# A place of its own for expert 60's weights: gate and up ahead of expert 3, down behind expert 11

## The chip, the core and the metric

One NeuronCore of a Trainium2 chip runs the kernel. Its engines are TensorE (PE), VectorE (DVE), ScalarE (ACT), GpSimd (POOL) and SyncE (SP); here SP does nothing but issue transfers. The metric is the device time of one execution in microseconds, as the median of the timed runs. One execution is taken apart by the profiler; its rows are quoted below.

## The reference

A two-layer trunk (layer 0 mixes with GLA, layer 1 with sparse attention), each layer followed by a mixture of 64 experts, for 256 prompt tokens and 8 samples. What matters here is the mixture: every token takes 8 of 64 experts, all weights are float32, and each expert is three matrices of 1 MB.

```python
N_EXPERTS = 64; TOP_K = 8; EXPERT_FF = 256; SHARED_FF = 256; D_MODEL = 1024

def swiglu(x, w_g, w_u, w_d):
    return (jax.nn.silu(x @ w_g) * (x @ w_u)) @ w_d

def moe_ffn(h, w_router, router_bias, w_gate, w_up, w_down, ws_gate, ws_up, ws_down):
    ...
    _, eidx = lax.top_k(jnp.where(emask, sel, -jnp.inf), TOP_K)
    wsel = jnp.take_along_axis(s, eidx, axis=-1)
    wsel = wsel / jnp.sum(wsel, axis=-1, keepdims=True) * ROUTE_SCALE
    y = routed_experts(x, eidx, wsel.astype(x.dtype), w_gate, w_up, w_down) + swiglu(x, ws_gate, ws_up, ws_down)

def reference(...):
    for i in range(DEPTH):                      # DEPTH = 2
        ...                                     # mixer, residual
        xp = xp + gt2p[:, None, :] * moe_ffn(modulate(xp, norm_ffn[i], sh2p, sc2p), *mo)
        xs = xs + gt2s[:, None, :] * moe_ffn(modulate(xs, norm_ffn[i], sh2s, sc2s), *mo)
    y_prompt = rms_norm(xp, norm_final)
    y_sample = rms_norm(xs, norm_final)
```

## The kernel before

Each engine runs its own program, written out in order; semaphores hold them together. In each layer a router picks the experts and makes, for each expert, a list of at most 64 tokens; tokens beyond that go to overflow chunks, which come in pairs after expert 63 (two pairs in layer 0, one in layer 1). An even and an odd expert form a pair: POOL gathers the pair's token rows (`gather`, L1828), TensorE transposes them (`pe_turn_half`, L1431), computes gate and up (L1484), transposes the product (L1496), computes down (L1510), and adds the pair before with one-hot matmuls (`pe_add`, L1439). A call of `pe_body` is one expert. Below, e58 is expert 58, and "expert 60 starts" means its first matmul of L1484.

The weights stream through `ring`, four slots (`WS = 4`) of three thirds of 2048 words per partition: gate, up, down. `load_expert` (L1233) issues three transfers on SP, one per third. `sp_experts_first` loads e0 to e3, each as soon as its slot is released by earlier work; the slot of e3 is the one that held the shared expert's weights, released at the end of the router (L1373). In `sp_experts` the load of expert n waits for expert n-4 to be done (semaphore `y`). All SP transfers stand in one queue, in the order of issue. In layer 1 the weight row of the final norm (`sp_final_weight`, L2617) is issued between the loads of e2 and e3.

`main_and_overflow` (L1522) is what TensorE, VectorE, ScalarE and GpSimd share: the first eight experts are unrolled (`apart = 2` rounds of four), then a loop takes four experts a round, then a loop takes the overflow pairs. In the unrolled part the token lists of later experts are still being made between the experts (`pe_between`, `dve_list`, `dve_sel`); the semaphore `lists` counts seven of them per layer.

TensorE waits for an expert's gate, up and down at one place, ahead of L1484:

```python
            wait_alone(pe, wsem, wval)
            gu = ring[:, s, 0:2, :].rearrange("p g (k n) -> p g k n", k=KT)
```

Gate and up lie next to each other in a slot, so one matmul of L1484 covers 128 columns of both (256 moving columns); the two halves of 64 output partitions alternate. In the trace each such float32 matmul stands as two records.

Of the kernel before, what the change touches and what calls it, by code (L numbers as in the profile page):

```python
# [24 lines left out]
P = 128  # L25
D = 1024
KT = D // P
# [5 lines left out]
NE, TOPK, NG, TOPG, FF = 64, 8, 8, 4, 256  # L33
CAP = 64
# [8 lines left out]
WS = 4  # L43
THIRD = 2048
# [110 lines left out]
def build(nc, ins, outs):  # L155
    ctx = ExitStack()
    with ctx:
# [5 lines left out]
        def S(name):  # L163
            if name not in sems:
                sems[name] = ctx.enter_context(nc.semaphore(name))
            return sems[name]
# [100 lines left out]
        def plan(n, signals=True, at=None):  # L267

            got = []
            for i in range(n):  # L270
                s = W.slot() if at is None else at[i % len(at)]
                W.loads[s] += 1
                prior[(s, W.loads[s])] = W.uses[s]
                W.uses[s] += signals
                got.append((s, W.loads[s]))
            return got
# [49 lines left out]
        it_sh = [plan(1)[0], None]  # L326
        after = [(it_sh[0][0] + i) % WS for i in range(1, WS)]
        it_ada[1] = plan(4, at=after)
        it_ex = [plan(NE, False, at=after[1:] + after[:1] + [it_sh[0][0]]), None]
        def hold(s):  # L330

            W.uses[s] += 1
# [6 lines left out]
        hold_v = hold(sd)  # L339
        it_dout = plan(2, at=[sb_, sa])  # L340
        it_sh[1] = plan(1, at=[sd])[0]
        it_ex[1] = plan(NE, False, at=[sb_, sc_, sa, sd])

        hk, hv = GH * GDK, GH * GDV
        w_in = ins["gla_w_in"][0]
# [836 lines left out]
        OH8 = [tk(DEC) for _ in range(2)]  # L1182
        iot = tk(TOK)
        Sel = arena[:, tk.at[0]:tk.at[0] + 1344].bitcast(BF16).rearrange("p (t m n) -> p t m n", t=TT, m=7)
        s_, sel, c1, c2, msk, rep = (tk(TT, NE) for _ in range(6))
        gm = tk(24, 8)
        Mf, Wt = tk(TT, NE), tk(TT, NE)
# [4 lines left out]
        Qall, Rall, Rres = tk(TT, NB), tk(TT, NB), tk(TT, NB)  # L1192
        MV = tk(NB, TT, 5, dt=BF16)
        QT, RT = tk(TT, P), tk(TT, P)
        cnt, nch, base, ovt = tk(1), tk(1), tk(1), tk(4)
        OV, OVb, OVc = tk(NOV), tk(NOV), tk(NOV)
        Lp = tk(NB // 2, 5)
# [26 lines left out]
        def M(l, name):  # L1224
            return S(f"{name}_{l}")
# [4 lines left out]
            return [wg.rearrange("(p k) n -> p (k n)", k=KT), wu.rearrange("(p k) n -> p (k n)", k=KT),  # L1230
                    wd.rearrange("(k p) n -> p k n", p=P)]

        def load_expert(s, e, l, sem):  # L1233
            for t, src in enumerate(expert_w(l, e)):
                dst = ring[:, s, t, :]
                if t == 2:
                    dst = dst.rearrange("p (k n) -> p k n", k=2)
                sp.dma_start(dst, src).then_inc(sem, 16)
# [13 lines left out]
        def sp_experts_first(l):  # L1252
            for u in range(WS):
                s, n = it_ex[l][u]
                sp.wait_ge(S(f"slot_used{s}"), prior[it_ex[l][u]])
                load_expert(s, u, l, S(f"slot_loaded{s}"))
                if l and u == 2:
                    sp_final_weight()

        def sp_experts(l):  # L1260
            with sp.Fori(1, NE // WS) as i:
                for u in range(WS):
                    s = it_ex[l][u][0]
                    sp.wait_ge(M(l, "y"), i * WS + (u - WS + 1))
                    load_expert(s, i * WS + u, l, S(f"slot_loaded{s}"))
            sp.wait_ge(S("lists"), PER["lists"] * l + 7)
            n2 = sp.value_load(npr[0:1, 0:1], min_val=1, max_val=NOV // 2)
            with sp.Fori(0, n2) as i:
                later = (i + 31) >> 5
                for u in range(2):  # L1270
                    e = sp.value_load(eid[0:1, ds(i * 2 + u, 1)], min_val=0, max_val=NE - 1)
                    sp.wait_ge(M(l, "y"), later * 2 + i * 2 + (NE - WS + u + 1))
                    load_expert(it_ex[l][u][0], e, l, M(l, f"over_loaded{u}"))
            sp.wait_ge(M(l, "y"), n2 * 2 + NE)


        def route_pe(eng, l, name):
# [190 lines left out]
        def pe_body(l, i, n, h2, u, s, wsem, wval, over):  # L1468

            b = u % 2  # L1470
            par = 1 if over else u // 2
            last = None if isinstance(h2, int) and h2 == 0 else h2 - 1

            def add(*chunks):
                if last is not None:
                    pe_add_pair(l, last, 1 if over else 1 - par, chunks, (1 if over else 4) in chunks)
            if b == 0:
                pe.wait_ge(M(l, "xgT"), h2 * 2 + 2)
            wait_alone(pe, wsem, wval)
            gu = ring[:, s, 0:2, :].rearrange("p g (k n) -> p g k n", k=KT)  # L1480
            rows = xgT[0 if over else par]
            for k in range(KT):
                for half in range(2):
                    m = pe.matmul(PS[64 * half:64 * half + 64, 5, 0:256].rearrange("p (g n) -> p g n", g=2), rows[:, k, CAP * b:CAP * b + CAP],  # L1484
                                  gu[:, :, k, half * P:(half + 1) * P], start=(k == 0), stop=(k == KT - 1), skip_group_check=True)
            m.then_inc(M(l, "gu"), 1)
            if isinstance(n, int):
                pe_between(l, n)
            if not over and b == 0:
                if isinstance(n, int):  # L1490
                    pe_bank6(l, n)
                pe_turn_half(l, h2 + 1, 1 - par, i + par, 0)
            elif not over:
                add(1)
            pe.wait_ge(M(l, "hm"), n + 1)
            pe.transpose(PS[:, 5, 256:384], hm[b], K["ident"]).then_inc(M(l, "th"), 1)  # L1496
            if over and b == 1:
                pe_turn_half(l, h2 + 1, 1, i + NE // 4, 0)
            elif over:
                add(4, 0)  # L1500
            elif b == 0:
                add(0)
            else:
                add(4)
            pe.wait_ge(M(l, "hT"), n + 1)
            if not isinstance(n, int) or n >= 1:
                pe.wait_ge(M(l, "ysb"), n)
            for kk in range(2):
                for j in range(2):
                    m = pe.matmul(PS[64 * j:64 * j + 64, 7, :], hTt[b][:, kk * CAP:(kk + 1) * CAP],  # L1510
                                  ring[:, s, 2, kk * D + 512 * j:kk * D + 512 * j + 512], start=(kk == 0), stop=(kk == 1), skip_group_check=True)
            m.then_inc(M(l, "y"), 1)
            if over and b == 0:
                add(1)
            elif over:
                pe_turn_half(l, h2 + 1, 1, i + NE // 4, 1)
            elif not over and b == 0:
                pe_turn_half(l, h2 + 1, 1 - par, i + par, 1)
# [3 lines left out]
        def main_and_overflow(eng, l, body, between=None):  # L1522

            for i in range(apart):
                for u in range(WS):
                    body(i, i * WS + u, i * 2 + u // 2, u, False)
            if between is not None:
                between()
            with eng.Fori(apart, NE // WS) as i:
                for u in range(WS):  # L1530
                    body(i, i * WS + u, i * 2 + u // 2, u, False)
            eng.wait_ge(S("lists"), PER["lists"] * l + 7)
            n2 = eng.value_load(npr[0:1, 0:1], min_val=1, max_val=NOV // 2)
            with eng.Fori(0, n2) as i:
                for u in range(2):
                    body(i, i * 2 + (NE + u), i + NE // 2, u, True)
            return n2

        def pe_experts(l):
            def body(i, n, h2, u, over):  # L1540
                s, first = it_ex[l][u]
                if over:
                    pe_body(l, i, n, h2, u, s, M(l, f"over_loaded{u}"), i * 48 + 48, over)
                else:
                    pe_body(l, i, n, h2, u, s, S(f"slot_loaded{s}"), i * 48 + 48 * first, over)
            pe_turn_half(l, 0, 0, 0, 0)
            pe_turn_half(l, 0, 0, 0, 1)
            n2 = main_and_overflow(pe, l, body, lambda: pe_bank6(l, WS * apart))
            pe.wait_ge(M(l, "xgT"), n2 * 2 + (NE + 2))
            if l:  # L1550
                pe_gates()
            wait_alone(pe, M(l, "ysb"), n2 * 2 + NE)
            pe.wait_ge(S("oh_last"), l + 1)
            pe_add_samples(OHw[:, SEQ:TOK], ysb[1]).then_inc(S("acc"), 1)
            pe_add(OHw, [ysb[1]], (0, 1)).then_inc(S("acc"), 1)
            if l:
                pe_final_rows(0)
            pe_add(OHw, [ysb[1]], (2, 3)).then_inc(S("acc"), 1)
# [1044 lines left out]
            act.wait_ge(S("kv_out"), 96)  # L2603


        wrow = shT.rearrange("p k t -> p (k t)")[:, 0:D]
        grow = ysb[0]
        xnew = [arena[:, D * i:D * i + D] for i in range(2)]
        row8 = arena[0:DEC, 2112:2112 + D]
# [5 lines left out]
        gate8 = modT2[:, 1, 40:48, 1:9]  # L2615

        def sp_final_weight():  # L2617
            sp.wait_ge(S("mix_out"), 16)
            sp.dma_start(wrow, ins["norm_final"].rearrange("(o n) -> o n", o=1).broadcast_to([P, D])).then_inc(S("dsa_in"), 16)

        def pe_gates():
# [223 lines left out]
```

## Time and profile before

| | us |
|---|---|
| timed runs, median of 3 | 1615.74 (1615.34 to 1617.96) |
| the profiled execution | 1616.23 |
| its span, first to last instruction | 1614.40 |
| PE busy | 1537.5 (95%) |
| DVE, ACT, POOL busy | 570.2, 438.7, 145.8 |
| bytes moved by DMA | 553.13 MB, mean 343 GB/s |

The page cuts the span into 40 slices of 40.4 us. The expert loop of layer 0 runs from about 271 to 806 us, that of layer 1 from about 1078 to 1593 us; the first is preceded by the GLA layer, the second by the attention layer. A busy PE is not PE at its peak, since matmuls are pipelined; the distance from one start to the next of the same kind of work says more than the busy share. DMA rows give the mean busy share of the 16 DMA engines (it can come out slightly over 1) and what they moved.

### The profile page before, as it was taken

To read this page: it belongs to the slowest core of one execution; us is meant where nothing else is said; L and a number is where in the kernel's file an instruction comes from. 1 tells how busy PE (TensorE), PEld (TensorE's weight loads), DVE (VectorE), ACT (ScalarE), POOL (GpSimd) and SP (SyncE) were. 2 spreads that over 40 slices of the span, in tenths; PEclk is the share of its full clock that TensorE was granted. 3 is DMA by queue.
4 is the path that set the end of the run, shared out by engine and by line. 5 is a ranking of instruction groups with operands and counts; after the bars stand their busy time and mean duration, and the time that the engine had idled before them with its cause. 6 is when DMAs were issued, how large, how long until landed. Compare 5 with 4: busy or idle time off the path is not lost.

```text
span 1614.4 us, 28531 instructions
## 1 busy us (share of the span) xinstructions
PE 1537.5 (95%) x10814; PEld 937.8 (58%) x10814; DVE 570.2 (35%) x1709; ACT 438.7 (27%) x975; POOL 145.8 (9%) x208
## 2 busy tenths in 40 slices
PE   5999999999999999999898989999999999999997
PEld 2768665555555555555477767765555555555554
DVE  4124554622122221212236972466222221212223
ACT  1211121222232222232232143312223222222223
POOL 0001301000000000000020051010000000000000
PEclk9999999999999999999999989999999999999999
DMA  9885678999999999999594656379999999999991
GB/s 368 339 343 190 248 286 335 386 402 416 416 417 416 416 416 416 417 415 414 211 328 105 183 169 202 138 277 390 413 417 416 417 416 416 416 417 416 415 410 75
DMA packets 132290, 553.13 MB, mean 343 GB/s; under 512 B 19503, under 2 KB 36861, under 8 KB 93830
## 3 DMA queue, kind: packets, MB, share of 16 engines
q1 hardware_dynamic: 113746, 514.28, 80.5%
q0 software_dynamic: 15472, 35.02, 6.0%
q10 hardware_dynamic: 3012, 3.00, 0.6%
q8 instruction: 41, 0.67, 0.2%
q14 instruction: 19, 0.16, 0.0%
HBM read 563.19 MB, written 8.96 MB: 354 GB/s over the span
## 4 chain that ended last, share of the span: by engine, by line
PE 70%; DMA 19%; DVE 6%; ACT 2%; issue 1%; SPq 1%; ACTq 1%; DVEq 0%
PE PS L1484 21%; DMA ring<-in_moe_w_down 19%; PE PS L1510 11%; PE PS L1439 6%; PE PS L783 5%; PE PS L943 4%; PE PS L1431 2%; PE PS L2046 2%; PE PS L2042 2%; PE PS L470 1%; PE PS L1446 1%; PE PS L1496 1%; PE PS L2098 1%; DVE arena L1714 1%; ACT arena L1796 1%
## 5 line engine op out<-in xcount | busy, mean ns | idle before, releaser
L1484 PE MATMUL PS<-ring,arena 128*64 128x256 f32 x4288 | 490.5, 381 | 13.1 <-DMA ring<-in_moe_w_down 8.2
L1484 PEld LDWEIGHTS PS<-ring,arena 128*64 128x64 f32 x4288 | 313.6, 137 | 188.5 <-issue 58.6
L1510 PE MATMUL PS<-ring,arena 128*64 128x512 f32 x1072 | 260.3, 606 | 1.4 <-ACT arena L1798 1.4
L1714 DVE TENSOR_TENSOR arena<-arena,PS 128x128 f32<-128x128 f32 x134 | 38.6, 288 | 500.1 <-ACT arena L1796 500.1
L1806 ACT COPY arena<-PS 64x512 f32<-64x512 f32 x134 | 77.5, 578 | 292.7 <-PE PS L1510 292.7
L1439 PE MATMUL PS<-y_parts,oh_pair 128*128 128x512 f32 x520 | 153.7, 417 | 0.0
L1702 DVE TENSOR_SCALAR y_parts<-arena 128x512 fp32r<-128x512 f32 x130 | 62.9, 483 | 247.3 <-ACT arena L1807 247.3
L1510 PEld LDWEIGHTS PS<-ring,arena 128*64 128x64 f32 x1072 | 65.2, 136 | 130.5 <-issue 100.6
L1796 ACT ACTIVATE arena<-PS 128x128 f32<-128x128 f32 x134 | 37.2, 278 | 338.8 <-PE PS L1484 338.8
L1431 PEld LDWEIGHTS PS<-cst,arena 128*128 128x128 f32 x552 | 71.8, 194 | 80.2 <-issue 78.3
L1826 POOL COPY arena<-arena 128x1 int32 (+1 forms) x71 | 15.0, 212 | 1093.4 <-PE PS L1431 909.0
L1439 PEld LDWEIGHTS PS<-y_parts,oh_pair 128*128 128x128 f32 x520 | 87.5, 188 | 38.8 <-issue 25.3
L1431 PE MATMUL PS<-cst,arena 128*128 128x128 f32 x552 | 97.7, 300 | 2.0 <-ACT arena L1813 1.4
L1704 DVE SCALAR_TENSOR_TENSOR y_parts<-arena,y_parts 128x512 fp32r<-128x512 f32 x130 | 97.7, 752 | 4.6
L783 PE MATMUL PS<-hT,ring 128*128 128x264 f32 x384 | 89.4, 390 | 0.4 <-DVE modT L511 0.4
L1813 ACT COPY arena<-PS 128x512 f32<-128x512 f32 x135 | 79.6, 590 | 26.1 <-PE PS L1431 24.5
L783 PEld LDWEIGHTS PS<-hT,ring 128*128 128x128 f32 x384 | 71.7, 190 | 19.2 <-issue 6.2
L1807 ACT COPY arena<-PS 64x512 f32<-64x512 f32 x134 | 78.0, 582 | 1.6
L1828 POOL DMA_INDIRECT arena<-h_rows,arena x71 | 72.5, 1021 | 61.7 <-POOL arena L1826 58.4
L1798 ACT COPY arena<-PS 128x128 f32<-128x128 f32 x134 | 35.7, 266 | 120.7 <-PE PS L1496 120.7
L943 PE MATMUL PS<-shT,ring 128*128 128x264 f32 x256 | 58.6, 390 | 1.6 <-PE PS L943 0.6
L943 PEld LDWEIGHTS PS<-shT,ring 128*128 128x128 f32 x256 | 48.8, 192 | 11.2 <-issue 1.4
(542 smaller groups left out, 1378.7 us busy)
## 6 DMA issues: line engine op xcount, KB each, us to landing
ring<-in_moe_w_gate SPq DMA_DIRECT2D x134, 1024.0 KB, 11.6
ring<-in_moe_w_up SPq DMA_DIRECT2D x134, 1024.0 KB, 15.9
ring<-in_moe_w_down SPq DMA_DIRECT2D x134, 1024.0 KB, 20.7
ring<-in_w_ada SPq DMA_DIRECT2D x36, 1024.0 KB, 12.4
ring<-in_gla_w_in SPq DMA_DIRECT2D x8, 1152.0 KB, 13.9
ring<-in_w_ada SPq DMA_DIRECT2D x8, 1152.0 KB, 11.9
ring<-in_dsa_w_in SPq DMA_DIRECT2D x6, 1024.0 KB, 20.8
arena<-in_state_gla POOLq DMA_DIRECT2D x8, 512.0 KB, 7.8
```

What stands on the lines that cost most here:

```text
L783: m = pe.matmul(PS[:, b, 0:TOK], w8_[:, k, (m_ % 6) * P:(m_ % 6 + 1) * P], hT[:, k, 0:TOK], start=(k == 0), stop=(k == KT - 1))
L943: m = pe.matmul(PS[:, 4 + k % 4, 0:TOK], w3[:, kk, (k % 2) * P:(k % 2 + 1) * P], src[:, kk, :], start=(kk == 0), stop=(kk == KT - 1))
L1431: ins_ = pe.transpose(PS[:, 6, k * P:(k + 1) * P], xv[:, 4 * half + k, :], K["ident"])
L1439: ins_ = pe.matmul(PS[:, c, :], oh[:, T * P:(T + 1) * P], y[:, 512 * j:512 * j + 512], start=False, stop=True, skip_group_check=True)
L1484: m = pe.matmul(PS[64 * half:64 * half + 64, 5, 0:256].rearrange("p (g n) -> p g n", g=2), rows[:, k, CAP * b:CAP * b + CAP], gu[:, :, k, ...
L1510: m = pe.matmul(PS[64 * j:64 * j + 64, 7, :], hTt[b][:, kk * CAP:(kk + 1) * CAP], ring[:, s, 2, kk * D + 512 * j:kk * D + 512 * j + 512], ...
L1702: dve.tensor_scalar(yR[:, 0, q], ysb[par][:, q], wv[:, par:par + 1], None, ALU.mult).then_inc(M(l, "part"), 1)
L1704: dve.scalar_tensor_tensor(out=yR[:, 1, q], in0=ysb[par][:, q], scalar=wv[:, par:par + 1], in1=yR[:, 0, q], op0=ALU.mult, op1=ALU.subtract ...
L1806: act.copy(ysb[par][q, 0:512], PS[0:CAP, 7, :])
L1807: act.copy(ysb[par][q, 512:D], PS[CAP:P, 7, :]).then_inc(M(l, "ysb"), 1)
L1813: act.copy(xgT[into][:, 4 * half:4 * half + 4, :].rearrange("p k c -> p (k c)"), bank(6)).then_inc(M(l, "xgT"), 1)
L1828: pool.indirect_dma_start(out=xg[into], out_offset=None, in_=hrow_d[l], in_offset=IndirectOffsetOnAxis(ap=gi[:, into:into + 1], axis=0), b ...
```

## The change

Expert 60 (`SPARE = NE - WS`) no longer goes through the ring. Its gate lies in the first 2048 words of `arena`, its up in the first 2048 of `shT`, its down in 2048 words of `arena` that held the router's temporaries (`spare`). Its transfers count on a semaphore of their own (`extra_loaded0`), gate and up are issued ahead of e3's slot wait (`sp_spare_in`), down behind the load of e11 (`sp_spare_down`). For that, SP's rounds for e4 to e11 are unrolled. e61 to e63 take the slots and waits that e60 to e62 had (`order`), the overflow pair takes slots 3 and 0 instead of 0 and 1 (`over_slot`). Since gate and up of e60 are not adjacent, each of its matmuls is split into one for gate and one for up, of 128 moving columns each. On the four compute engines e60 to e63 are unrolled. The final norm's row, in layer 1, moves from behind e2's load to behind e60's down, and from `shT` to another part of `arena`.

```diff
-        it_ex = [plan(NE, False, at=after[1:] + after[:1] + [it_sh[0][0]]), None]
+        SPARE = NE - WS
+        order = lambda e: e - 1 if e > SPARE else e
+        it_ex = [plan(NE - 1, False, at=after[1:] + after[:1] + [it_sh[0][0]]), None]
...
+        spare = [arena[:, 0:THIRD], shT.rearrange("p k t -> p (k t)")[:, 0:THIRD], arena[:, routed_at:routed_at + THIRD]]
...
-        def load_expert(s, e, l, sem):
-            for t, src in enumerate(expert_w(l, e)):
-                dst = ring[:, s, t, :]
+        def load_expert(s, e, l, sem, thirds=range(3)):
+            for t in thirds:
+                dst, src = spare[t] if s is None else ring[:, s, t, :], expert_w(l, e)[t]
...
                 s, n = it_ex[l][u]
+                if u == WS - 1:
+                    sp_spare_in(l)
                 sp.wait_ge(S(f"slot_used{s}"), prior[it_ex[l][u]])
                 load_expert(s, u, l, S(f"slot_loaded{s}"))
-                if l and u == 2:
-                    sp_final_weight()
+
+        def sp_spare_in(l):
+
+            route_pe(sp, l, "e_T")
+            sp.wait_ge(S("mix_out"), KT * (l + 1))
+            load_expert(None, SPARE, l, M(l, "extra_loaded0"), (0, 1))
+
+        def sp_spare_down(l):
+
+            sp.wait_ge(S("lists"), PER["lists"] * l + 7)
+            load_expert(None, SPARE, l, M(l, "extra_loaded0"), (2,))
+            if l:
+                sp_final_weight()
 
         def sp_experts(l):
-            with sp.Fori(1, NE // WS) as i:
+            def load(i, u):
+                sp.wait_ge(M(l, "y"), i * WS + (u - WS + 1))
+                s = it_ex[l][u][0]
+                load_expert(s, i * WS + u, l, S(f"slot_loaded{s}"))
+            for i in range(1, 3):
                 for u in range(WS):
-                    s = it_ex[l][u][0]
-                    sp.wait_ge(M(l, "y"), i * WS + (u - WS + 1))
-                    load_expert(s, i * WS + u, l, S(f"slot_loaded{s}"))
+                    load(i, u)
+            sp_spare_down(l)
+            with sp.Fori(3, NE // WS - 1) as i:
+                for u in range(WS):
+                    load(i, u)
+            for e in range(SPARE + 1, NE):
+                s = it_ex[l][order(e)][0]
+                sp.wait_ge(M(l, "y"), order(e) - WS + 1)
+                load_expert(s, e, l, S(f"slot_loaded{s}"))
...
-                    sp.wait_ge(M(l, "y"), later * 2 + i * 2 + (NE - WS + u + 1))
-                    load_expert(it_ex[l][u][0], e, l, M(l, f"over_loaded{u}"))
+                    sp.wait_ge(M(l, "y"), later * (2 if u else 3) + i * 2 + (NE - WS + 2 * u))
+                    load_expert(over_slot(l, u), e, l, M(l, f"extra_loaded{u}"))
             sp.wait_ge(M(l, "y"), n2 * 2 + NE)
+
+        def over_slot(l, u):
+            return it_ex[l][(NE - 1 + u) % WS][0]
...
             for k in range(KT):
+                if s is None:
+                    for g in range(2):
+                        for half in range(2):
+                            m = pe.matmul(PS[64 * half:64 * half + 64, 5, P * g:P * g + P], rows[:, k, CAP * b:CAP * b + CAP],
+                                          gu[g][:, k, half * P:(half + 1) * P], start=(k == 0 and g == 0), stop=(k == KT - 1), skip_group_check=True)
+                    continue
...
-            with eng.Fori(apart, NE // WS) as i:
+            with eng.Fori(apart, NE // WS - 1) as i:
                 for u in range(WS):
                     body(i, i * WS + u, i * 2 + u // 2, u, False)
+            for u in range(WS):
+                body(NE // WS - 1, SPARE + u, SPARE // 2 + u // 2, u, False)
...
-        wrow = shT.rearrange("p k t -> p (k t)")[:, 0:D]
+        wrow = arena[:, routed_at + THIRD:routed_at + THIRD + D]
...
         def sp_final_weight():
-            sp.wait_ge(S("mix_out"), 16)
```

## Rows read from the trace of the kernel before

**Rows 1.** The page, parts 1 and 2: busy times; GB/s in 40 slices.
```profile
PE 1537.5 (95%) x10814; PEld 937.8 (58%) x10814; DVE 570.2 (35%) x1709; ACT 438.7 (27%) x975; POOL 145.8 (9%) x208
...
GB/s 368 339 343 190 248 286 335 386 402 416 416 417 416 416 416 416 417 415 414 211 328 105 183 169 202 138 277 390 413 417 416 417 416 416 416 417 416 415 410 75
```

**Rows 2.** Timeline of PE (start us, us long, line, form), layer 0, e14 to e16.
```profile
382.09 3.62 PE L1484 MATMUL PS<-ring,arena 128*64 128x256 f32 x32
...
390.20 3.67 PE L1484 MATMUL PS<-ring,arena 128*64 128x256 f32 x32
...
397.35 2.98 PE L1484 MATMUL PS<-ring,arena 128*64 128x256 f32 x26
```

**Rows 3.** Timeline of PE, layer 0, e58 to e62; brackets: idle before, what ended it.
```profile
725.54 3.67 PE L1484 MATMUL PS<-ring,arena 128*64 128x256 f32 x32 [0.19 <-issue]
...
733.73 3.67 PE L1484 MATMUL PS<-ring,arena 128*64 128x256 f32 x32
...
741.37 3.67 PE L1484 MATMUL PS<-ring,arena 128*64 128x256 f32 x32 [0.32 <-DMA ring<-in_moe_w_down]
...
749.55 3.67 PE L1484 MATMUL PS<-ring,arena 128*64 128x256 f32 x32
...
756.70 3.62 PE L1484 MATMUL PS<-ring,arena 128*64 128x256 f32 x32
```

**Rows 4.** Windows, layer 0: stretch, its length, busy by engine, PE clock, DMA share, GB/s.
```profile
276.00:280.00 4.00, 3.98 (x26) 2.04 (x28) 3.53 (x9) 2.20 (x4) 0.84 (x1) 1.00 0.62 208
...
304.00:308.00 4.00, 4.00 (x36) 2.25 (x32) 2.86 (x4) 1.16 (x2) 0.00 (x0) 1.00 0.58 192
308.00:336.00 28.00, 27.94 (x247) 15.76 (x245) 14.73 (x46) 7.81 (x18) 1.98 (x4) 1.00 1.00 403
336.00:366.00 30.00, 29.88 (x212) 16.28 (x210) 7.25 (x18) 8.97 (x20) 3.15 (x5) 1.00 1.01 401
366.00:742.00 376.00, 369.55 (x2556) 203.44 (x2554) 86.89 (x216) 108.50 (x242) 28.68 (x48) 1.00 1.02 416
```

**Rows 5.** DMA issues of the whole run: size of each, median us to landing.
```profile
ring<-in_moe_w_gate SPq DMA_DIRECT2D x134, 1024.0 KB, 11.6
...
shT<-in_norm_final SPq DMA_DIRECT2D x1, 512.0 KB, 18.7
```

**Rows 6.** Timeline of SP's issues, layer 1: the norm's row, then e3's first.
```profile
1047.19 0.52 SPq L2619 DMA_DIRECT2D shT<-in_norm_final  x1
1074.81 0.33 SPq L1238 DMA_DIRECT2D ring<-in_moe_w_gate  x1
```

**Rows 7.** Windows, layer 1, columns as in rows 4.
```profile
1068.00:1075.00 7.00, 6.67 (x32) 2.84 (x30) 5.48 (x12) 0.00 (x0) 0.00 (x0) 1.00 0.01 2
1142.00:1532.00 390.00, 383.81 (x2654) 211.48 (x2652) 90.36 (x225) 112.89 (x252) 29.95 (x51) 1.00 1.02 416
```

**Rows 8.** Timeline of PE, layer 1, e58 to e61.
```profile
1531.59 3.67 PE L1484 MATMUL PS<-ring,arena 128*64 128x256 f32 x32 [0.46 <-DMA ring<-in_moe_w_down]
...
1539.74 3.67 PE L1484 MATMUL PS<-ring,arena 128*64 128x256 f32 x32
...
1547.16 3.67 PE L1484 MATMUL PS<-ring,arena 128*64 128x256 f32 x32
...
1555.34 3.67 PE L1484 MATMUL PS<-ring,arena 128*64 128x256 f32 x32
```

**Rows 9.** Timeline of PE, attention layer: 64 weight columns, 128 moving, alternating halves.
```profile
874.43 3.76 PE L2123 MATMUL PS<-arena 128*64 128x128 f32 x64 [1.12 <-ACT arena L2540]
```

**Rows 10.** e61's down: SP's issue; then size and us to landing (DMA issues, 725 to 727.5).
```profile
726.43 0.38 SPq L1238 DMA_DIRECT2D ring<-in_moe_w_down  x1
...
ring<-in_moe_w_down SPq DMA_DIRECT2D x1, 1024.0 KB, 22.4
```

**Rows 11.** Waits from 540 to 760 us: us in total, times, longest.
```profile
PE PS L1484 <- issue: 3.1, 6, 1.3
```

**Rows 12.** Timeline of PE: the router's transposes of layer 1.
```profile
1043.87 0.37 PE L1308 MATMUL PS<-cst,arena 64*128 64x64 f32 x3
```

More of the change, by code:

```diff
@@ L341, in build @@
         it_sh[1] = plan(1, at=[sd])[0]
-        it_ex[1] = plan(NE, False, at=[sb_, sc_, sa, sd])
+        it_ex[1] = plan(NE - 1, False, at=[sb_, sc_, sa, sd])
         hk, hv = GH * GDK, GH * GDV
@@ L1184, in build @@
         Sel = arena[:, tk.at[0]:tk.at[0] + 1344].bitcast(BF16).rearrange("p (t m n) -> p t m n", t=TT, m=7)
+        routed_at = tk.at[0]
+        spare = [arena[:, 0:THIRD], shT.rearrange("p k t -> p (k t)")[:, 0:THIRD], arena[:, routed_at:routed_at + THIRD]]
         s_, sel, c1, c2, msk, rep = (tk(TT, NE) for _ in range(6))
@@ L1194, in build @@
         QT, RT = tk(TT, P), tk(TT, P)
+        assert tk.at[0] >= routed_at + THIRD + D
         cnt, nch, base, ovt = tk(1), tk(1), tk(1), tk(4)
@@ L1479, in pe_body @@
             wait_alone(pe, wsem, wval)
-            gu = ring[:, s, 0:2, :].rearrange("p g (k n) -> p g k n", k=KT)
+            gu = ([spare[g].rearrange("p (k n) -> p k n", k=KT) for g in range(2)] if s is None
+                  else ring[:, s, 0:2, :].rearrange("p g (k n) -> p g k n", k=KT))
+            wd = spare[2] if s is None else ring[:, s, 2, :]
             rows = xgT[0 if over else par]
             for k in range(KT):
+                if s is None:
[4 more added lines that the diff above has]
+                    continue
                 for half in range(2):
@@ L1510, in pe_body @@
                     m = pe.matmul(PS[64 * j:64 * j + 64, 7, :], hTt[b][:, kk * CAP:(kk + 1) * CAP],
-                                  ring[:, s, 2, kk * D + 512 * j:kk * D + 512 * j + 512], start=(kk == 0), stop=(kk == 1), skip_group_check=True)
+                                  wd[:, kk * D + 512 * j:kk * D + 512 * j + 512], start=(kk == 0), stop=(kk == 1), skip_group_check=True)
             m.then_inc(M(l, "y"), 1)
@@ L1542, in body @@
                 if over:
-                    pe_body(l, i, n, h2, u, s, M(l, f"over_loaded{u}"), i * 48 + 48, over)
+                    pe_body(l, i, n, h2, u, over_slot(l, u), M(l, f"extra_loaded{u}"), i * 48 + (48 if u else 96), over)
+                elif isinstance(n, int) and n == SPARE:
+                    pe_body(l, i, n, h2, u, None, M(l, "extra_loaded0"), 48, over)
+                elif isinstance(n, int) and n > SPARE:
+                    s, nth = it_ex[l][order(n)]
+                    pe_body(l, i, n, h2, u, s, S(f"slot_loaded{s}"), 48 * nth, over)
                 else:
```

## The prediction

> **What bounds the kernel now.** I read the page's busy times and slices first, then the timeline of TensorE at three places of the expert loops, then windows of the DMA engines, then the issues on SP. The page [rows 1] gives TensorE 95% of the span, and slices 9 to 18 and 28 to 38 move 415 GB/s or so: through both expert loops two resources are full at once, and the question is which of them ends last at each expert.
>
> In the middle of a loop it is TensorE. From one expert's first gate/up matmul to the next it takes 8.11 us after an even expert and 7.15 us after an odd one [rows 2], 15.26 us for a pair, and nothing is waited for. The weights come more slowly: an expert is three transfers of 1024 KB [rows 5], and with the gathered token rows between them the queue, at a flat 416 GB/s from 366 to 742 us [rows 4], does not keep up. So the lead that the four slots had at the start is used up, and later each even expert waits a little for its down weights: e58 to e60 of layer 0 take 8.19 and 7.64 us, 15.83 for the pair [rows 3].
>
> What is decisive is where that ends. After e60 the strides are 8.18 and 7.15 us [rows 3], those of TensorE alone. Expert 60 is the last one that the stream delays; from there to the loop's end the time is TensorE's own. Layer 1 is the same: 7.42 us from e59 to e60, 8.18 to e61, with a wait ahead of e58 [rows 8].
>
> **The change, part by part.** Times are set against the profiled execution, 1616.23 us with a span of 1614.40; the median of the timed runs is 0.49 us lower.
>
> *Bytes moved.* At 416 GB/s a transfer of 1024 KB costs 1,048,576 / 416,000 = 2.52 us, one of 512 KB 1.26 us. Expert 60's gate and up (5.04 us of stream) go ahead of e3's load, its down (2.52 us) behind e11's, and in layer 1 the final norm's row (512 KB, 1.26 us [rows 5]) goes from ahead of e3 to behind that down. All experts from e12 to e59 are behind these in one queue. Let d be by how much later their weights land. What was e60's turn in the queue is now e61's, so e61 and all behind it come some 5 us earlier against their need; but there TensorE sets the pace, and nothing is won by it.
>
> *d in layer 1.* SP issues the norm's row at 1047.19 and then nothing until 1074.81 [rows 6]; from 1068 to 1075 us the DMA engines move 2 GB/s [rows 7]. Gate and up need 5.04 us of that and the row leaves it, so they are free. Down and the row land in a stretch (1142 to 1532 us) that runs at 416 GB/s without a hole [rows 7]: d = 2.52 + 1.26 = 3.78 us. Below, I bound it by 2.52, if the row, one line read for all partitions, should cost nothing.
>
> *d in layer 0.* Here e3 follows e2 closely, so gate and up push e3 back; e3 has time, and what counts is which holes they fill later. Measured as bytes missing to 416 GB/s, the windows 276 to 280 and 304 to 308 us hold 4 x (1 - 208/416) = 2.00 and 4 x (1 - 192/416) = 2.15 us; 308 to 336 holds 0.87 and 336 to 366 1.08 us; after that, nothing [rows 4]. If a deeper queue wins all of it back, gate and up are absorbed by 336 (5.02 of 5.04 us) and of the down 2.52 - 1.08 = 1.44 us stay: d = 1.46. If only the idle share of the two holes counts, 4 x (1 - 0.62) + 4 x (1 - 0.58) = 3.20 us, d = 7.56 - 3.20 = 4.36. I take the two holes in full and half of the two shallow windows, because in these the engines are already busy and only the rate is low: d = 7.56 - 4.15 - 0.98 = 2.4 us.
>
> *What d does at the end.* The last expert that waits is now e58, since e60's weights are there. It starts d later; e59 follows as before, e60 at TensorE's 7.15 us. Against before, the waits ahead of e60 and e61 are gone: 7.64 - 7.15 and 8.18 - 8.11, 0.56 us in layer 0 [rows 2, 3]; 7.42 - 7.15 and 8.18 - 8.11, 0.34 us in layer 1 [rows 2, 8].
>
> *Two-piece matmuls.* Expert 60's gate and up are no longer side by side, so 16 matmuls of 256 columns become 32 of 128, 64 records in place of 32. The trace has just this form, 64 columns of weights on alternating halves with 128 moving columns: 64 records in 3.76 us [rows 9], against 3.67 us for the 32 [rows 2]. That is 0.09 us a layer, all on TensorE's path. The Trainium skill (TensorE: Matmul & The Clock Gate, Back-to-back issue gap) speaks against such a split: sustained, it gives about 81 ns a matmul at 128 columns, because weight loading then sets the spacing. By that, an estimate from the page, 64 records would take 5.2 us and the change would cost 1.5 us a layer more than the 3.67; the row with the same form decides here.
>
> *Unrolling and waits.* Four bodies a layer stand unrolled on each engine and one round of the loop goes; I cost it at nothing, since it is the same instructions. Below nothing there is no room: across the loop's turn, from e15 to e16, the stride is the bare 7.15 us [rows 2]. From above I take the longest idle time ahead of a gate/up matmul that the trace leaves to issue, 1.3 us [rows 11], once a layer. SP's new waits are met before it comes to them. Gate and up wait for the router's transposes (L1308), in layer 1 at 1043.87 us, and SP is there at 1047.19 [rows 6, 12]; were they late, e3's load would stand behind. The down's is for the last of the seven lists, which VectorE makes within e7's body, while e11's load, ahead of it on SP, waits until e7 is done; were it late, e12's load would stand behind it. The overflow loads move from slots 0 and 1 to 3 and 0; the second pair's first load still waits for the first pair's first expert.
>
> *Sum.* Layer 0: 2.4 - 0.56 + 0.09 = +1.93 us. Layer 1: 3.78 - 0.34 + 0.09 = +3.53 us. Together +5.5 us: 1621.7 for the profiled execution, **1621.2 us** for the median, 0.34% slower. With both lower ends (1.46 and 2.52) it is +3.3 us, with the upper one (4.36) and 1.3 us a layer for issue +10.0.
>
> **The rivals.**
>
> *The stream sets the end, and the change is faster.* If what follows e60 hangs on the stream and not on TensorE, each layer gains what left the busy part: 5.04 us less what layer 0 cannot absorb, and 5.04 - 1.26 in layer 1, up to 8.8 us: 1606.9 us. For it: e61's down is issued at 726.43 and lands 22.4 us later, 0.7 us before e61 starts [rows 3, 10], so after e60 both are close. Against it: being early by 0.7 us is not being late, and the strides are the bare ones of rows 2. The point from which it decides is a wait ahead of e62 or later; there is none. Chance 0.10.
>
> *The waits are a round trip and not a rate, and nothing changes.* Each wait of the loop could be that of four slots: a slot is released, and its new weights land 22 us later, whatever else is queued. Then one more transfer behind e11 delays nobody (d = 0), and the loss of the waits at e60 gives -0.56 - 0.34 + 0.18 = -0.7 us: 1615.0 us. The Trainium skill (Perfetto Trace Analysis, Optimization Strategy) has this reading: a gap that repeats can mean that there are too few buffers for the next tile. By that rule a fifth home is the right remedy; the trace disagrees here, with 416 GB/s whether experts wait or not. Against it speaks that flat rate [rows 4, 7]: the queue is full, and a full queue passes a delay on. Chance 0.10. Another 0.10 for within 0.2% comes from the lower ends of the forecast.
>
> *Slower by more.* The unrolled tail stalls on its code, or split matmuls cost more than the row says: 1624.5 us and beyond. Chance 0.08. The forecast itself, above 0.2%, has 0.62.
>
> **How the numbers follow.** About 0.2%, 3.2 us, is what a measurement of this kernel can tell from no change. Faster by more: 0.10. Within: 0.10 + 0.10 = 0.20. Slower by more: 0.62 + 0.08 = 0.70. The forecast's own range is 1619.0 to 1624.5. The range for 8 in 10 takes in the round-trip case and leaves out the faster rival and what lies above: 1615.0 to 1624.5.
>
> **What would show it.** Right: e58 still waits for its down weights and starts some 2.4 us (layer 0) and 3.8 us (layer 1) later against the loop's first expert; the first waits come at an earlier expert of each loop; e60 to the loop's end runs at 7.15 and 8.1 us with weights landed long before; expert 60's gate/up take 3.8 us. Wrong: e58 not later, which is the round trip; strides under 7.15 us after e60, which is the faster rival; a gap between the loop and e60, which is code.

## The result and the profile after

| | before | after |
|---|---|---|
| median of 20 runs each, us | 1617.17 (1612.5 to 1622.0) | 1622.55 (1615.4 to 1626.54) |
| ratio, with its 95% interval | | 1.0033 (1.0022 to 1.0044) |
| profiled execution, and its span, us | 1616.23, 1614.40 | 1620.23, 1618.4 |

The change makes the kernel 0.33% slower: 5.4 us by the medians, 3.6 to 7.1 by the interval. The prediction was 1621.2 us, 5.5 us over the median of three runs of before that it started from (1615.74); twenty runs put that median at 1617.17. It was right, and the runs below say how far for its reasons.

The page of after, parts 1 and 2, beside [rows 1]: TensorE is as busy as before, and both loops still move 415 to 417 GB/s once they are under way. Fuller are above all the slices around the loops' starts, counted from 0 as in the prediction: 6 and 7 (366 and 403 GB/s for 335 and 386) and 26 and 27 (318 and 397 for 277 and 390).

```profile
PE 1537.6 (95%) x10878; PEld 939.9 (58%) x10878; DVE 569.4 (35%) x1709; ACT 438.7 (27%) x975; POOL 146.1 (9%) x208
...
GB/s 369 336 344 190 247 288 366 403 407 417 416 417 416 417 416 417 416 415 390 169 326 109 179 169 216 144 318 397 405 417 416 417 416 416 416 416 417 415 377 32
```

SP's issues in after (start us, us, line): gate and up of expert 60, then e3's first load, in layer 0 and in layer 1. They go out 8.8 us before e3's in layer 0 and 27.7 us before it in layer 1.

```profile
259.25 0.39 SPq L1243 DMA_DIRECT2D arena<-in_moe_w_gate  x1
259.68 1.22 SPq L1243 DMA_DIRECT2D shT<-in_moe_w_up  x1
268.06 0.33 SPq L1243 DMA_DIRECT2D ring<-in_moe_w_gate  x1
...
1047.56 0.41 SPq L1243 DMA_DIRECT2D arena<-in_moe_w_gate  x1
1048.01 0.46 SPq L1243 DMA_DIRECT2D shT<-in_moe_w_up  x1
1075.24 0.33 SPq L1243 DMA_DIRECT2D ring<-in_moe_w_gate  x1
```

Windows of after, columns as in [rows 4]. The two early holes of layer 0 are nearly gone (411 and 369 GB/s for 208 and 192), the idle stretch of layer 1 moves 83 GB/s for 2, and the long stretches stand at 416 as before [rows 4, 7].

```profile
276.00:280.00 4.00, 3.65 (x23) 1.77 (x24) 3.88 (x11) 2.32 (x5) 0.84 (x1) 1.00 1.01 411
...
304.00:308.00 4.00, 4.00 (x34) 2.25 (x32) 3.27 (x5) 1.16 (x2) 0.00 (x0) 0.99 0.96 369
308.00:336.00 28.00, 27.94 (x247) 15.76 (x245) 14.73 (x46) 7.81 (x18) 1.74 (x3) 1.00 0.99 393
336.00:366.00 30.00, 29.89 (x212) 16.34 (x210) 7.24 (x18) 8.97 (x20) 3.40 (x5) 1.00 1.02 413
366.00:742.00 376.00, 368.25 (x2544) 203.48 (x2540) 86.83 (x216) 107.62 (x240) 28.68 (x48) 1.00 1.02 416
...
1068.00:1075.00 7.00, 7.00 (x32) 3.00 (x30) 5.86 (x13) 0.00 (x0) 0.00 (x0) 1.00 0.22 83
...
1142.00:1532.00 390.00, 381.62 (x2634) 211.32 (x2631) 90.28 (x225) 111.83 (x249) 30.37 (x51) 1.00 1.02 416
```

TensorE's timeline in after (L1523 is gate/up from the ring, L1519 the two-piece form of e60): e58 to e63 of layer 0, then e58 and e59 of layer 1.

```profile
728.53 3.67 PE L1523 MATMUL PS<-ring,arena 128*64 128x256 f32 x32
...
736.69 3.67 PE L1523 MATMUL PS<-ring,arena 128*64 128x256 f32 x32
...
743.84 0.39 PE L1519 MATMUL PS<-arena 128*64 128x128 f32 x4
744.05 0.39 PE L1519 MATMUL PS<-shT,arena 128*64 128x128 f32 x4
...
747.11 0.39 PE L1519 MATMUL PS<-shT,arena 128*64 128x128 f32 x4
...
751.90 3.67 PE L1523 MATMUL PS<-ring,arena 128*64 128x256 f32 x32
...
759.05 3.62 PE L1523 MATMUL PS<-ring,arena 128*64 128x256 f32 x32
...
767.07 3.67 PE L1523 MATMUL PS<-ring,arena 128*64 128x256 f32 x32
...
1535.33 3.67 PE L1523 MATMUL PS<-ring,arena 128*64 128x256 f32 x32 [0.26 <-DMA ring<-in_moe_w_down]
...
1543.49 3.67 PE L1523 MATMUL PS<-ring,arena 128*64 128x256 f32 x32
```

e58 is late and still held up: its start lies 7.46 us behind e57's in layer 0 and 7.58 in layer 1, where the bare stride is 7.15, and the row of layer 1 names the down. Behind e60 the strides of layer 0 are bare, 8.06, 7.15 and 8.02 us, and e60 itself follows e59 by 7.15. Set against the loop's first gate/up matmul (before at 270.71 and 1077.83 us, after at 271.11 and 1078.26), in us:

| | layer 0 | layer 1 |
|---|---|---|
| e58 starts, before, after | 454.82, 457.42 | 453.76, 457.07 |
| later by (predicted d) | 2.60 (2.4) | 3.31 (3.78) |
| last overflow expert starts, before, after | 528.96, 530.78 | 509.16, 512.05 |
| later by (predicted) | 1.82 (1.93) | 2.89 (3.53) |

The first expert whose start is held up by more than 0.2 us moves from e38 to e28 in layer 0 and from e34 to e24 in layer 1. The whole span is 4.0 us longer: 0.40 ahead of the first loop, 1.82 in it, 1.78 less between the loops, 2.89 in the second loop, 0.70 behind its last expert. The 1.78 lie between the last expert of layer 0 and the first of layer 1, where the change moves only transfers. Over the nine kernels of this document that stretch takes 272.6 to 278.2 us, before has the longest, and the granted clock differed: 0.91 before and 0.87 after from 800 to 840 us, 0.91 and 1.00 from 840 to 860, 0.91 and 0.94 from 900 to 960, which is, as an estimate, -1.6 + 1.8 + 1.8 = 2.0 us of work. The 0.70 belong to the change, by its unrolled bodies; the experiments show it.

### The profile page after: what moved, and what is told of

Its sections match the earlier page's. It is cut to its first block, busy times and chain, and to the rows that moved or that the text cites. A ratio compares the mean times of both kernels' runs of the same rounds, so it can differ in the third digit from the quotient of the medians.

```text
span 1618.4 us, 28449 instructions
## 1 busy us (share of the span) xinstructions
PE 1537.6 (95%) x10878; PEld 939.9 (58%) x10878; DVE 569.4 (35%) x1709; ACT 438.7 (27%) x975; POOL 146.1 (9%) x208
## 4 chain that ended last, share of the span: by engine, by line
PE 64%; DMA 25%; DVE 6%; ACT 2%; issue 1%; SPq 1%; ACTq 1%; DVEq 0%
DMA ring<-in_moe_w_down 25%; PE PS L1523 18%; PE PS L1549 10%; PE PS L1470 6%; PE PS L785 5%; PE PS L945 4%; PE PS L2092 2%; PE PS L2088 2%; PE PS L1462 2%; PE PS L472 1%; PE PS L1535 1%; PE PS L1477 1%; SPq L1243 1%; PE PS L2144 1%; DVE arena L1760 1%
## 5 line engine op out<-in xcount | busy, mean ns | idle before, releaser
L1523 PE MATMUL PS<-ring,arena 128*64 128x256 f32 x4224 | 483.5, 381 | 16.8 <-DMA ring<-in_moe_w_down 12.0
L1523 PEld LDWEIGHTS PS<-ring,arena 128*64 128x64 f32 x4224 | 310.2, 137 | 189.4 <-issue 63.3
L1549 PE MATMUL PS<-ring,arena 128*64 128x512 f32 x1056 | 256.5, 606 | 1.4 <-ACT arena L1844 1.4
L1549 PEld LDWEIGHTS PS<-ring,arena 128*64 128x64 f32 x1056 | 64.2, 136 | 128.8 <-issue 98.9
L785 PEld LDWEIGHTS PS<-hT,ring 128*128 128x128 f32 x384 | 71.7, 190 | 19.2 <-issue 6.2
```

Of the source, the lines that this page charges most:

```text
L785: m = pe.matmul(PS[:, b, 0:TOK], w8_[:, k, (m_ % 6) * P:(m_ % 6 + 1) * P], hT[:, k, 0:TOK], start=(k == 0), stop=(k == KT - 1))
```

## The experiments

Two readings are drawn on in each: the ratio of timed runs, and one row of part 5 of each profile's page, the gate/up group. Its columns are line, engine, form and count, then us busy and mean ns of one, then us of idle time ahead of it and how much of that ended with a landing transfer. Before and after read:

```profile
L1484 PE MATMUL PS<-ring,arena 128*64 128x256 f32 x4288 | 490.5, 381 | 13.1 <-DMA ring<-in_moe_w_down 8.2
```

```profile
L1523 PE MATMUL PS<-ring,arena 128*64 128x256 f32 x4224 | 483.5, 381 | 16.8 <-DMA ring<-in_moe_w_down 12.0
```

The change has 3.7 us more of idle time there, 3.8 us more of waiting for down weights. Differences of 1 to 2 us in this row say little: the kernel that changes no weight transfer ("Only the unrolling", below) is 1.5 us over before in both.

**The down (and the norm's row) issued late.** Expert 60's down and the norm's row go out behind e59's load, where nobody waits for the queue; all the rest of the change stays (the first overflow load waits one expert longer, as in before).

```diff
-            sp_spare_down(l)
             with sp.Fori(3, NE // WS - 1) as i:
                 for u in range(WS):
                     load(i, u)
+            sp_spare_down(l)
             for e in range(SPARE + 1, NE):
```

> The changed kernel, but expert 60's down and the norm's row are issued behind e59's load instead of behind e11's (and the first overflow load waits one expert longer, as in the kernel before). Theory (the queue is full from e12 on, and only bytes ahead of e58 in it count): e58 no later against e0 than in the kernel before, 0 to +1.2 us in layer 0 (what of gate and up is not absorbed early), 0 in layer 1; e60 without its wait, 0.5 and 0.3 us earlier. In all -1.5 to +0.5 us to the kernel before, some 5.5 us under the changed kernel. Round trip (the bytes behind e11 delay nobody, the loss lies in the split matmuls, the unrolled tail or elsewhere): e58 as in the changed kernel, time still about +5 us.

Measured: 1616.82 us, ratio 0.9998 (0.9979 to 1.0018). The loss is gone, by moving two issues on SP. The row agrees:

```profile
L1523 PE MATMUL PS<-ring,arena 128*64 128x256 f32 x4224 | 484.7, 382 | 13.5 <-DMA ring<-in_moe_w_down 8.8
```

The split matmuls, the unrolled bodies and the new slots are all still there, so together they cost nothing that the timing can see. Its profile alone would not have said so: e58 starts 1.03 us later than in before in layer 0, and 3.26 us later in layer 1, where 0 was expected and the change has 3.31. The last section puts the 3.26 down to the granted clock at the start of that loop.

**One transfer more.** The kernel before, with one extra 1024 KB transfer behind e11's load in each layer, into memory that nothing reads there. To place it, SP's rounds for e4 to e11 are unrolled as in the change (not shown below), and TensorE's wait for the first overflow chunk counts the extra transfer.

```diff
+            sp.wait_ge(S("lists"), PER["lists"] * l + 7)
+            sp.dma_start(arena[:, routed_at:routed_at + THIRD].rearrange("p (k n) -> p k n", k=2), expert_w(l, NE - WS)[2]).then_inc(M(l, "over_loaded0"), 16)
             with sp.Fori(3, NE // WS) as i:
```

> The kernel before, with one transfer of 1024 KB more per layer behind e11's load, into memory that is dead there; nothing reads it. Theory (full queue): e58, e60 and all behind later by 2.5 us in layer 1 and by 1.4 to 2.5 us in layer 0, together +4 to +5 us, about 1621. Round trip: the extra transfer passes beside the waits, 0 us.

Measured: 1621.26 us, ratio 1.0039 (1.0024 to 1.0055). The transfer alone brings a loss as large as the whole change. e58 starts 2.61 us later in layer 0 and 2.18 in layer 1, for the 2.52 us that 1024 KB take at 416 GB/s.

```profile
L1492 PE MATMUL PS<-ring,arena 128*64 128x256 f32 x4288 | 490.8, 381 | 16.6 <-DMA ring<-in_moe_w_down 11.9
```

This takes the round-trip rival away: each expert has the slots that it had before, and the time grows by about what the extra bytes take. The unrolled rounds on SP are in the version above too, which loses nothing. The Trainium skill (Perfetto Trace Analysis, Optimization Strategy) offers too few buffers as a reading of a gap that repeats; here the trace disagrees, since the gaps grew by 3.5 us, and the time by 3.9 us or more, with the number of buffers unchanged.

**All three transfers behind e11.** Gate and up of expert 60 lose their place in the holes.

```diff
-                if u == WS - 1:
-                    sp_spare_in(l)
...
             load_expert(None, SPARE, l, M(l, "extra_loaded0"), (2,))
+            sp_spare_in(l)
```

> The changed kernel with expert 60's gate and up behind e11's load too, together with its down. Theory: layer 1 loses the 5.04 us that found idle engines ahead of e3, layer 0 what found holes up to 336 us; d = 7.56 + 1.26 in layer 1 and 7.56 - 1.08 in layer 0, less 0.34 and 0.56: +14.4 us to the kernel before, about 1631. Rival (early transfers are paid anyway, since in layer 0 they push e3 back): layer 0 as in the changed kernel, +10 us.

Measured: 1633.15 us, ratio 1.0093 (1.0067 to 1.0119), 15 us over before. The order of issue alone, with the same bytes, is worth some 10 us against the change as made. So gate and up were nearly free where the change put them, and the delay grows with the bytes at about the rate of the stream. The rival had layer 0 as in the changed kernel; e58 of layer 0 starts 5.73 us later than there, which speaks against it, and +10 us lies just outside the interval (10.8 to 19.2 us).

```profile
L1522 PE MATMUL PS<-ring,arena 128*64 128x256 f32 x4224 | 485.8, 382 | 25.0 <-DMA ring<-in_moe_w_down 18.4
```

**The norm's row alone moved late.** Only the 512 KB row goes behind e59's load; the down stays behind e11.

```diff
             load_expert(None, SPARE, l, M(l, "extra_loaded0"), (2,))
-            if l:
-                sp_final_weight()
...
+            if l:
+                sp_final_weight()
             for e in range(SPARE + 1, NE):
```

> The changed kernel with the norm's row alone issued behind e59's load; down stays behind e11's. Theory: -1.26 us to the changed kernel, all in layer 1, so some +4 us to the kernel before. Rival (the row costs nothing in the stream): +5.4 us as the changed kernel.

Measured: 1620.86 us, ratio 1.002 (1.0002 to 1.0039). The interval, 0.3 to 6.3 us, holds both expectations, so the time does not settle what the row costs. e58 of layer 1 starts 0.58 us earlier than in after, where 1.26 were expected; in the pair of kernels with the home for e12 (below) the same move gives 1.00 us. That the row costs stream time is likely by these two and not shown: in layer 0, where this kernel and after run the same program, e58 starts 1.08 us earlier too.

**Only the unrolling.** The kernel before with e60 to e63 unrolled on the compute engines. Its weights move as in before.

```diff
-            with eng.Fori(apart, NE // WS) as i:
+            with eng.Fori(apart, NE // WS - 1) as i:
                 for u in range(WS):
                     body(i, i * WS + u, i * 2 + u // 2, u, False)
+            for u in range(WS):
+                body(NE // WS - 1, NE - WS + u, (NE - WS) // 2 + u // 2, u, False)
```

> The kernel before with e60 to e63 unrolled on the compute engines, weights as before. Theory: at most 0.1 us an even expert (8.11 to about 8.0), -0.3 us in all, nothing that timing sees. Rival (the unrolled tail stalls on its code): a gap ahead of e60 or e61, up to +2.6 us.

Measured: 1616.91 us, ratio 0.9998 (0.9978 to 1.0017): between -3.6 and +2.7 us. Its row:

```profile
L1484 PE MATMUL PS<-ring,arena 128*64 128x256 f32 x4288 | 492.2, 382 | 14.6 <-DMA ring<-in_moe_w_down 9.7
```

The stall of the rival is not there: e59 to e60 takes 7.60 us in layer 0, where before has 7.64, and 7.15 in layer 1. The trace holds two small effects of opposite sign. Unrolled even experts take 8.02 to 8.07 us in place of 8.11. And the span ends 0.7 us later behind the last expert: the distance from the last overflow expert's gate/up to the end is 28.08 to 28.09 us in all five kernels whose last four experts are unrolled, 27.37 to 27.42 in the other four. In each of the five, and in none of the four, the DMA queues of the last microseconds hold one packet of the instruction queue beside the outputs. In after, 1612 to 1619 us (queue: packets, MB, share):

```profile
q1 hardware_dynamic: 304, 1.08, 42.0%
q14 instruction: 1, 0.01, 0.3%
```

So the 0.7 us come with the unrolling. That they are a wait for this packet is argued from the coincidence; no run changed it by itself.

**The home given to expert 12.** If only bytes ahead of a waiting expert count, the home should serve the first expert behind e11: its gate and up then fill the holes, its down lands where it would have anyway, and all behind are early by what the holes took. `SPARE = 12`; SP's loads and the bodies of e12 to e15 are unrolled accordingly, and e13 to e63 take the slot of the expert before; e60 to e63 are back in the loop.

```diff
-        SPARE = NE - WS
+        SPARE = 12
...
             sp_spare_down(l)
-            with sp.Fori(3, NE // WS - 1) as i:
+            for e in range(SPARE + 1, SPARE + 8):
+                s = it_ex[l][order(e)][0]
+                sp.wait_ge(M(l, "y"), e - 4 if e < SPARE + 5 else e - 3)
+                load_expert(s, e, l, S(f"slot_loaded{s}"))
+            with sp.Fori(5, NE // WS) as i:
                 for u in range(WS):
-                    load(i, u)
-            for e in range(SPARE + 1, NE):
-                s = it_ex[l][order(e)][0]
-                sp.wait_ge(M(l, "y"), order(e) - WS + 1)
-                load_expert(s, e, l, S(f"slot_loaded{s}"))
+                    s = it_ex[l][(u - 1) % WS][0]
+                    sp.wait_ge(M(l, "y"), i * WS + (u - WS + 1))
+                    load_expert(s, i * WS + u, l, S(f"slot_loaded{s}"))
```

> The change with expert 12 in the home instead of expert 60: gate and up ahead of e3, down behind e11, that is in e12's own turn; e0 to e15 unrolled instead of e0 to e7 and e60 to e63; the norm's row stays behind e11. Theory (what counts is how many bytes stand in the queue ahead of the experts that wait): from e13 on the stream lacks e12's gate and up, so e58 and e60 come earlier, by 3.2 to 5.0 us in layer 0 (what gate and up find of early holes) and by 5.04 - 1.26 = 3.8 us in layer 1; in all -7 to -9 us, 1608 to 1610. Round trip: a home more or less changes no wait, 0 us; and if the loss of the changed kernel lies in split matmuls or SP's extra waits, +5 us as there.

Measured: 1609.89 us, ratio 0.9954 (0.9936 to 0.9972). It is faster than both kernels, by 7.4 and some 12.7 us. Waits for down weights fall to 4.5 us, and the first held-up expert moves to e50 in layer 0 and e46 in layer 1. The unrolled bodies can hardly be the cause: four even experts a layer are shorter by about 0.1 us each, under 1 us in all, and they lie ahead of the waits. The row:

```profile
L1525 PE MATMUL PS<-ring,arena 128*64 128x256 f32 x4224 | 484.2, 382 | 8.6 <-DMA ring<-in_moe_w_down 4.5
```

**The same with the norm's row late.** The row goes behind the last expert's load.

```diff
             load_expert(None, SPARE, l, M(l, "extra_loaded0"), (2,))
-            if l:
-                sp_final_weight()
...
+            if l:
+                sp_final_weight()
             sp.wait_ge(S("lists"), PER["lists"] * l + 7)
```

> Expert 12 in the home, as in the run before, and the norm's row issued behind the last expert's load instead of behind e11's. Theory (bytes ahead of the waiting experts): layer 1 gains the row's 1.26 us more, in all -8 to -10 us to the kernel before, some 1.3 us under the version with the row behind e11. Rival (the row, one line read for all partitions, takes no share of the stream): no difference between the two.

Measured: 1608.16 us, ratio 0.9949 (0.9924 to 0.9974), the lowest of all. Its lead over the version above lies inside both intervals; e58 of layer 1 starts 1.00 us earlier than there.

**All runs at one clock.** Single runs of one kernel differ by some 15 us (before: 1608.7 to 1624.3), more than the effects looked for. Most of that goes with the mean granted clock of the run, 0.984 to 0.993. Fitting one slope to the 144 timed runs of the nine kernels, and a level of its own to each kernel, gives -1.31 us per 0.001 of clock (standard error 0.09) and leaves a scatter of 2.1 us, where before alone scatters by 3.6. The size is plausible: 0.001 of the mean clock is 0.002 of 1615 us at 1.2 in place of 2.4 GHz, 3.2 us with 1.6 us of work lost. The fit alone does not show that the clock is the cause. The 20 runs of after are set here against the 53 runs of before from the two sessions of the experiments, since no clock is on record for those of its own session. At equal clock the kernels stand to before as follows, us with 95% bounds:

| kernel | at equal clock | predicted or expected |
|---|---|---|
| after | +4.5 ± 1.1 | +5.5 |
| down and row late | -0.8 ± 1.3 | -1.5 to +0.5 |
| one transfer more | +4.2 ± 1.3 | +4 to +5 |
| all three behind e11 | +15.9 ± 1.8 | +14.4 |
| row alone late | +3.2 ± 1.3 | some +4 |
| unrolling alone | -1.1 ± 1.4 | about -0.3 |
| home for e12 | -7.5 ± 1.3 | -7 to -9 |
| home for e12, row late | -8.4 ± 1.7 | -8 to -10 |

## Why the prediction was right, step by step

**What bounds the loops.** Right. The stream moves 414 to 416 GB/s from 366 to 742 and from 1142 to 1532 us in every kernel tried, and transfers issued ahead of the waiting experts delay them by about their bytes. By the table, one of 1024 KB in each layer costs 4.2 us, three in each layer (and the row in layer 1) cost 15.9, and with the late ones behind e59 the loss is gone. This is also why a fifth home for e60 could not help: those that wait are among e12 to e59, and it takes no byte out of their way.

**d.** Right in its mechanism, and in its size as far as the profiles tell: 2.60 for 2.4 us in layer 0, 3.31 for 3.78 in layer 1. The kernel with only the row moved late runs layer 0 with the program of after and has 1.52 there, so 0.2 or 0.5 us are within what one profile leaves open. The bytes are a second reading. Windows from 46 us ahead of each loop's first gate/up matmul to 100 us behind it, layer 0 and 1, columns as in [rows 4], before and then after:

```profile
224.71:370.71 146.00, 142.30 (x1108) 83.23 (x1101) 74.41 (x231) 37.64 (x79) 11.89 (x18) 0.99 0.95 379
1031.83:1177.83 146.00, 138.87 (x1075) 84.88 (x1074) 77.89 (x246) 41.13 (x86) 11.80 (x18) 1.00 0.84 331
```

```profile
225.11:371.11 146.00, 142.27 (x1108) 83.22 (x1101) 74.37 (x231) 37.61 (x79) 11.90 (x18) 0.99 0.98 394
1032.26:1178.26 146.00, 138.87 (x1075) 84.86 (x1074) 77.88 (x246) 41.13 (x86) 11.81 (x18) 1.00 0.86 342
```

The change put 7.56 us of stream ahead of e12 in each layer. After takes back 146 x 15 / 416 = 5.3 us in layer 0 and 146 x 11 / 416 = 3.9 in layer 1, which leaves 2.3 and 3.7 us, for 2.60 and 3.31 us in the timeline. These rates are rounded to 1 GB/s, 0.35 us each. The choice of the holes in full and half of the shallow windows, 5.1 us won back, came close to the 5.3, in part by luck. In the windows of [rows 4] the two holes gave back (411 - 208) x 4 / 416 = 1.95 and (369 - 192) x 4 / 416 = 1.70 us in place of 4.15, and the shallow windows -0.67 + 0.87 = 0.20 in place of 0.98. Part of what made it up lies earlier: the 11 us ahead of the loop, which the sum did not have, gave (419 - 388) x 11 / 416 = 0.82, before and after:

```profile
259.71:270.71 11.00, 9.23 (x42) 4.34 (x41) 4.52 (x8) 1.17 (x2) 0.18 (x1) 1.00 1.00 388
260.11:271.11 11.00, 9.20 (x43) 4.32 (x41) 4.47 (x8) 1.17 (x2) 0.18 (x1) 1.00 1.02 419
```

The hole at 304 to 308 us is itself no fixed part of the loop: it stands behind a fall of the granted clock (last section).

**The lost waits.** Right. From e58 to e61 after takes 0.65 us less in layer 0 and 0.36 in layer 1, for 0.56 - 0.09 and 0.34 - 0.09 predicted. Both are a little larger, since the next two terms are smaller.

**The split matmuls.** Cheaper than taken. From 743.84 to 747.50 us the 64 records take 3.66 us, what the 32 of 256 columns take [rows 2], so 0.0 us in place of 0.09. That is 57 ns a record. The 81 ns of the Trainium skill (TensorE: Matmul & The Clock Gate, Back-to-back issue gap) do not hold for this form; by them the row would have been 5.2 us.

**Unrolling.** The step had it at nothing, with no room below. Two things are there: an unrolled even expert is 0.04 to 0.09 us shorter than one in the loop, which the stride of an odd expert across the loop's turn could not show; and the span's end is 0.7 us later. The bound of 1.3 us a layer from above is larger than that, but it was meant for a gap ahead of gate and up and not for the end. The stall that the rival of a slower kernel named, between the loop and e60, is not there: e59 to e60 takes 7.15 us in both layers.

**Where chance helped.** The sum was made for the loops, 5.46 us; the two loops of the profiled pair give 1.82 + 2.89 = 4.71. The agreement of 5.5 with 5.4 us to a tenth is luck: the interval is 3.6 to 7.1, and at equal clock the change costs 4.5 us. In the profiled pair, what the loops fell short and the 0.7 us at the end that no term named nearly cancel. The range has a flaw as well: its upper end in the sum, +10.0 us, is 1625.7 us, and the 1624.5 that stands there is not derived from it; the result lies below both. The rivals: the stream does not set the end, since the strides behind e60 are TensorE's in both layers; the round trip is refuted by the one extra transfer; and neither the split matmuls nor a stall in the unrolled tail made it slower by more.

## What to carry to other kernels

In a queue that is full, a place to prefetch into is worth only what it takes out of the queue ahead of a consumer that waits: fill the idle stretch at the start, and give the place to an early consumer behind it, not to the last. Of the two places tried here, the same memory cost 0.33% as a home for expert 60 and gained 0.46 to 0.51% as a home for expert 12. Before moving a transfer, list who stands behind it and waits; a transfer that is needed late should also be issued late.

## What the runs showed of the hardware

**A short fall of the clock at a loop's start is paid again at its end.** In five of the nine profiles the first expert of layer 1's loop runs partly at the lower level, and so does a second stretch some 30 us later. TensorE's timeline and windows of the kernel with the late down (columns as in [rows 4]):

```profile
1076.70 5.21 PE L1523 MATMUL PS<-ring,arena 128*64 128x256 f32 x32 [0.77 <-ACT arena L1859]
```

```profile
1066.00:1072.00 6.00, 6.00 (x15) 2.66 (x14) 5.69 (x14) 0.00 (x0) 0.00 (x0) 1.00 0.36 139
1072.00:1076.00 4.00, 2.92 (x27) 1.57 (x25) 0.61 (x1) 0.62 (x2) 0.00 (x0) 1.00 0.32 78
1076.00:1080.00 4.00, 3.30 (x17) 2.13 (x19) 0.00 (x0) 0.55 (x1) 1.20 (x2) 0.57 1.01 427
...
1106.00:1112.00 6.00, 6.00 (x34) 3.10 (x35) 4.65 (x12) 0.27 (x1) 0.00 (x0) 0.72 0.95 389
1112.00:1114.00 2.00, 2.00 (x20) 1.26 (x18) 1.63 (x3) 1.16 (x2) 0.00 (x0) 1.00 0.59 115
```

The same stretches of before stay at 1.00:

```profile
1072.00:1076.00 4.00, 3.34 (x26) 1.49 (x24) 1.73 (x2) 0.28 (x1) 0.00 (x0) 1.00 0.21 25
1076.00:1080.00 4.00, 2.88 (x24) 2.30 (x26) 0.00 (x0) 0.89 (x2) 1.20 (x2) 1.00 0.85 344
...
1106.00:1112.00 6.00, 6.00 (x48) 3.34 (x49) 5.05 (x13) 1.42 (x3) 0.00 (x0) 1.00 0.96 386
1112.00:1114.00 2.00, 2.00 (x28) 1.18 (x25) 1.89 (x3) 0.13 (x1) 0.00 (x0) 1.00 0.97 373
```

A granted clock of 0.57 over 4 us is mostly the level of 1.2 GHz, and e0's gate/up takes 5.21 us in place of 3.67. Ahead of the first fall TensorE had been busy throughout and then idle for a part (2.92 of 4 us busy); ahead of the second, from 1106 us, it was busy without a gap. Before has much the same idle stretch (3.34 and 2.88 of 4 us) without a fall, so the rows don't say what tips it. TensorE's work takes longer there, and SP's next load goes out later, 35.6 us behind the loop's first matmul in place of 32.7 (issues at 1112.31 and 1110.56 us): 115 GB/s from 1112 to 1114 us in place of 373. The stream is full from there on and can't make it up. The kernel with only the unrolling has the same weight transfers as before and the same falls; in the aligned window of layer 1 it moves 322 GB/s for 331:

```profile
1033.82:1179.82 146.00, 138.94 (x1056) 84.10 (x1057) 76.00 (x240) 40.05 (x83) 11.81 (x18) 0.98 0.81 322
```

That is 146 x 9 / 416 = 3.2 us of stream, and e58 starts 2.99 us later than in before, 400 us after the clock is back. With this kernel as the measure in layer 1, among profiles with the falls, e58 comes 0.27 us later with the late down (0 expected), 8.85 later with all three behind e11 (8.82), 3.79 earlier with the home for e12 (3.78), and 4.79 earlier with the row late as well (5.04). Set against before and its own expected d, e58 of layer 1 is off by -0.5 to +0.2 us in the three others without the falls (after, one transfer more, row alone late), and 3.0 to 3.3 us late in all five with them. So a single profile can't tell 1 us of a change in a loop that hangs on the stream, unless the clock of its first stretches is compared too.

Layer 0 has such a fall some 30 us into its loop in eight of the nine profiles, before among them; the hole of [rows 4] from 304 to 308 us follows it. The ninth, with the row alone late, has no fall and no hole there: 415 GB/s, for 369 in after, which runs the same program up to there. Before, then the kernel with the row late, whose loop starts 3.2 us later:

```profile
300.00:304.00 4.00, 4.00 (x19) 1.31 (x19) 3.79 (x11) 0.27 (x1) 0.00 (x0) 0.57 1.01 411
304.00:308.00 4.00, 4.00 (x36) 2.25 (x32) 2.86 (x4) 1.16 (x2) 0.00 (x0) 1.00 0.58 192
```

```profile
303.00:307.00 4.00, 4.00 (x29) 1.78 (x30) 3.79 (x12) 0.75 (x2) 0.00 (x0) 1.00 1.02 415
307.00:311.00 4.00, 4.00 (x55) 2.82 (x51) 3.72 (x8) 0.95 (x3) 0.00 (x0) 1.00 1.03 415
```

**Left open.** In layer 0 e58 of the kernel with only the unrolling is 2.14 us later than in before with 379 GB/s in both aligned windows. The windows of its loop account for less than 1 us of that, and what delays it was not found.
